# A block pair with 16 experts on one core: the router taken chunk by chunk from unscaled rows, the first expert job written out, and the high half's buffer given back after the high pass

## What is computed

```python
h = h + (g_conv * y_conv + g_sgu * y_sgu) @ w_out          # output projection
t = rms_norm(h, norm_ffn_g)                                # t = h / rms(h) * gain
p_group = softmax(t @ w_rg + b_rg)                         # 4 groups
pg, g_idx = top_k(p_group, 1)
exp_logits = t @ w_re + b_re                               # 16 experts, 4 in a group
sel = exp_logits of the chosen group; the best 2 of softmax(sel), normalised
gate = pg * those weights
hid = silu(t @ w_gate[e]) * (t @ w_up[e])                  # D_EXPERT = 512
y = sum over e of (hid * gate[:, e]) @ w_down[e]
out = rms_norm(h + y, norm_final_g)
```

## Time and profile before

| what | value |
|---|---|
| median of 3 runs | 2387.46 us (2387.45 to 2388.37) |
| the profiled execution, its time | 2387.44 us |
| its span | 2385.7 us |
| TensorE busy | 2328.2 us (98%) |
| VectorE busy | 1625.7 us (68%) |
| ScalarE busy | 1219.7 us (51%) |
| GpSimd busy | 185.5 us (8%) |
| mean granted TensorE clock | 0.984 |
| bytes moved | 510.90 MB, mean 214 GB/s |

### The profile page before, as it was taken

How to read it: one execution, slowest core, us unless ns; L and a number is a source line. 1 busy time by engine, 2 the same in 40 slices (tenths; PEclk the granted TensorE clock), 3 DMA queues, 4 the chain that set the end, 5 groups by cost and what they waited for, 6 DMA issues and landing times.

```text
span 2385.7 us, 35385 instructions
## 1 busy us (share of the span) xinstructions
PE 2328.2 (98%) x12313; PEld 1985.9 (83%) x12313; DVE 1625.7 (68%) x1904; ACT 1219.7 (51%) x1217; POOL 185.5 (8%) x71
## 2 busy tenths in 40 slices
PE   9999899999999999999999999999979999999997
PEld 9999688888888878888888888887867877778776
DVE  2999666555566554445586655575558888888887
ACT  4443346444444434444543544443446776767666
POOL 4676001000000000000100000000000000000000
PEclk9999899999999999999999999999979999999999
DMA  7655256667667655554676666654529989899895
GB/s 195 168 151 173 65 193 172 184 191 192 185 186 193 188 164 193 193 193 159 197 213 190 173 187 186 183 175 171 193 73 342 359 306 371 322 343 349 316 370 209
DMA packets 445235, 510.90 MB, mean 214 GB/s; under 512 B 12252, under 2 KB 407156, under 8 KB 410100
## 3 DMA queue, kind: packets, MB, share of 16 engines
q1 hardware_dynamic: 443812, 504.30, 65.6%
q0 software_dynamic: 1104, 5.78, 0.7%
q10 hardware_dynamic: 272, 0.20, 0.0%
HBM read 508.15 MB, written 2.10 MB: 214 GB/s over the span
## 4 chain that ended last, share of the span: by engine, by line
PE 93%; DVE 3%; ACT 2%; issue 2%; DVEq 0%; ACTq 0%; POOL 0%; POOLq 0%
PE ps L1925 24%; PE ps L1843 16%; PE ps L1930 13%; PE ps L2109 9%; PE ps L2125 7%; PE ps L2113 5%; PE ps L1753 3%; PE ps L1754 3%; PE ps L1776 2%; PE ps L2001 2%; ACT whi L553 1%; PE ps L1856 1%; PE ps L2090 1%; DVE wlo L988 1%; PE ps L1693 1%
## 5 line engine op out<-in xcount | busy, mean ns | idle before, releaser
L988 DVE TENSOR_TENSOR wlo<-raw,whi 128x2048 fp32r<-128x2048 f32 x440 | 1007.3, 2290 | 291.2 <-ACT whi L553 290.0
L553 ACT ACTIVATE whi<-raw 128x2048 fp32r<-128x2048 f32 x476 | 911.6, 1916 | 536.3 <-PE ps L1843 214.8
L1925 PE MATMUL ps<-xT,whi 128*128 128x512 f32 x2656 | 638.1, 391 | 5.2 <-DVE xT L1390 4.3
L1925 PEld LDWEIGHTS ps<-xT,whi 128*128 128x128 f32 x2656 | 487.7, 189 | 99.5 <-issue 4.4
L1930 PEld LDWEIGHTS ps<-xT,wlo 128*128 128x128 f32 x2656 | 343.2, 191 | 14.3
L1930 PE MATMUL ps<-xT,wlo 128*128 128x256 f32 x2656 | 347.4, 283 | 0.0
L733 ACT ACTIVATE wk<-ps 128x256 f32<-128x256 f32 x184 | 68.8, 383 | 451.5 <-PE ps L1930 451.5
L1843 PE MATMUL ps<-whi,act 128*128 128x512 f32 x1120 | 270.4, 394 | 2.8 <-ACT act L650 2.8
L2109 PE MATMUL ps<-whi,moe_r 128*128 128x512 f32 x1024 | 258.5, 395 | 6.0 <-ACT whi L553 6.0
L1843 PEld LDWEIGHTS ps<-whi,act 128*128 128x128 f32 x1120 | 213.5, 191 | 50.4 <-ACT act L650 3.7
L2109 PEld LDWEIGHTS ps<-whi,moe_r 128*128 128x128 f32 x1024 | 191.8, 189 | 49.8 <-ACT whi L553 7.6
(11 more groups left out here) (285 smaller groups left out, 1838.0 us busy)
## 6 DMA issues: line engine op xcount, KB each, us to landing
raw<-in_w_in SPq DMA_DIRECT2D x72, 1024.0 KB, 5.5
raw<-in_w_exp_gate SPq DMA_DIRECT2D x64, 1024.0 KB, 4.8
raw<-in_w_exp_up SPq DMA_DIRECT2D x64, 1024.0 KB, 4.8
raw<-in_w_exp_down SPq DMA_DIRECT2D x64, 1024.0 KB, 4.8
raw<-in_ffn_w_gate SPq DMA_DIRECT2D x44, 1024.0 KB, 5.6
raw<-in_ffn_w_up SPq DMA_DIRECT2D x44, 1024.0 KB, 5.5
raw<-in_ffn_w_down SPq DMA_DIRECT2D x44, 1024.0 KB, 4.8
raw<-in_conv_w_in SPq DMA_DIRECT2D x32, 1024.0 KB, 6.0
```

What stands on the lines that cost most here:

```text
L553: fn(whi[:, s % 2, :], raw[:, s % RING, :], ACT.Copy).then_inc(hi_ready, 1)
L988: V.tensor_tensor(wlo[:, s % 2, :], raw[:, s % RING, :], whi[:, s % 2, :], ALU.subtract).then_inc(lo_ready, 1)
L1925: mm(ps[:, bank, :], whi[:, s % 2, at:at + P], xT5[:, k0 + k, :], start=(k == 0), stop=False)
```

## The change

- The router's weights are multiplied once by the gain of the norm (`wr_scaled`; the gain comes as columns with one more small transfer at the start). The logits are then made from the unscaled `h`, and the reciprocal root is applied to the 20 logits with the bias, on VectorE, after them.
- `h` is turned chunk by chunk (`turn_tokens`) into the bank just added; those of token block 0 and the first logits stand between the chunks of the output projection's last pair (`between`). Copies of block 0 are VectorE's, of block 1 ScalarE's. Squares are taken by chunks.
- GpSimd multiplies `h` by the gain into `tmp` (eight chunks); ScalarE and VectorE split these into `tH` and `tL` by chunks with the reciprocal root as a scale (`token_hi`, `token_lo`), at four places of their order.
- `fill(6)` puts six 128-column matmuls of ones after the logits and six after the ranks.
- The first job is written out before the loop, which now is `Fori(1, jobs)`. It has no scatter, no result to split, no `take`. Its gathers use four banks, and its first four panels start as each chunk of `xg` is there. The experts' choice is spread between its panels; the loop's count is computed after panel 8 and loaded after the job. The body common to all jobs is `job_rest`.
- `expert_hi` takes the place of `hi` for all expert panels but the first two of a job: it waits for the end of the high pass of panel s-2 (new semaphore `whi_used`) and for its `lo`, not for `mm_done`. `expert_lo` waits in addition for `mm_done` of panel s-2, whose low half it overwrites.

```diff
+            def expert_hi(n, s):
+                a.wait_ge(whi_used, n + (s - 1 - MOE))
+                a.wait_ge(lo_ready, n + (s - 1 - B))
+                a.wait_ge(raw_in[s % RING], n * 4 + (16 * (s // RING) + 16))
+                fn(whi[:, s % 2, :], raw[:, s % RING, :], ACT.Copy).then_inc(hi_ready, 1)
+            def expert_lo(n, s):
+                v.wait_ge(mm_done, n + (s - 1))
+                lo(n, s)
...
 in_panel:
                 for o in range(2):
                     for k in range(4):
-                        mm(ps[:, bank, :], xg[:, o, 4 * q + k, :], whi[:, s % 2, k * DE:(k + 1) * DE],
-                           start=(q == 0 and o == 0 and k == 0), stop=False)
+                        i = mm(ps[:, bank, :], xg[:, o, 4 * q + k, :], whi[:, s % 2, k * DE:(k + 1) * DE],
+                               start=(q == 0 and o == 0 and k == 0), stop=False)
+                i.then_inc(whi_used, 1)
                 pe.wait_ge(lo_ready, n + (s + 1 - B))
...
 GpSimd:
-            pool.wait_ge(mm_done, MOE)
+            pool.wait_ge(mm_done, G)
             pool.iota(...); pool.memset(SelT ...)
+            pool.wait_ge(gain_in, 96)
+            for t in range(TOK):
+                for c in range(NC):
+                    pool.wait_ge(add_done, 16 + t * NC + c + 1)
+                    pool.tensor_tensor(tmp[:, t, c * BANK:(c + 1) * BANK], h[:, t, c * BANK:(c + 1) * BANK],
+                                       gB[:, c * BANK:(c + 1) * BANK], ALU.mult).then_inc(xn_ready, 1)
...
 ScalarE, router:
+            for c in range(NC):
+                row_square(0, c)
+            for c in range(NC):
+                row_square(1, c)
+                if c == 0:
+                    row_root(0)
+                if c == NC - 1:
+                    row_root(1)
+                a.wait_ge(tt_turned, NC + c + 1)
+                fn(tiles[:, 4 * c:4 * c + 4, P:2 * P], ps[:, 4 + c, :]..., ACT.Copy).then_inc(tt_ready, 1)
+            token_hi(0)
+            token_hi(1)
+            hi(MOE, 0)
+            token_hi(2)
+            gathered(0, 0, FIRST_ROWS[0])
+            token_hi(3)
+            gathered(0, 1, FIRST_ROWS[1])
+            gathered_hi(0, 0, FIRST_TURN[0])
+            hi(MOE, 1)
+            gathered(0, 2, FIRST_ROWS[2])
+            gathered_hi(0, 1, FIRST_TURN[1])
+            gathered(0, 3, FIRST_ROWS[3])
+            gathered_hi(0, 2, FIRST_TURN[2])
+            expert_hi(MOE, 2)
+            gathered_hi(0, 3, FIRST_TURN[3])
+            expert_hi(MOE, 3)
+            expert_hi(MOE, 4)
+            (two Exp) expert_hi(MOE, 5)
+            silu_gate(MOE + 4)
+            expert_hi(MOE, 6)
+            expert_hi(MOE, 7)
+            job_rest(0, MOE)
...
 VectorE, router:
+            for c in range(NC):
+                row_add(0, c)
+            for c in range(NC):
+                row_add(1, c)
+                if c == 1:
+                    row_sum(0)
+                if c == 2:
+                    row_scale(0)
+                v.wait_ge(tt_turned, c + 1)
+                V.tensor_copy(tiles[:, 4 * c:4 * c + 4, 0:P], ps[:, c, :]...).then_inc(tt_first, 1)
+            row_sum(1)
+            row_scale(1)
...
+            for t in range(TOK):
+                V.scalar_tensor_tensor(out=lg[:, t, :], in0=ps[:, t, 0:NL], scalar=st[:, RS + t:RS + t + 1], in1=brow[:, :],
+                                       op0=ALU.mult, op1=ALU.add)
             (mask)
+            token_lo(0)
             (ranks, slots, select(0))
+            token_lo(1)
+            token_lo(2)
+            gathered_lo(0, 0, FIRST_TURN[0])
+            lo(MOE, 0)
+            token_lo(3)
+            gathered_lo(0, 1, FIRST_TURN[1])
+            lo(MOE, 1)
+            gathered_lo(0, 2, FIRST_TURN[2])
+            gathered_lo(0, 3, FIRST_TURN[3])
+            expert_lo(MOE, 2)
             chosen_logits()
+            expert_lo(MOE, 3)
             chosen_experts()
+            expert_lo(MOE, 4)
+            expert_lo(MOE, 5)
+            silu_gate(1)
             chosen_gates()
+            expert_lo(MOE, 6)
+            expert_lo(MOE, 7)
+            expert_lo(MOE, 8)
+            overflow()
+            job_rest(0, MOE)
...
 TensorE:
+            row_stage(G, S_G, KT, first_rows)      # first_rows(c): turn_tokens(0, c); from c = 2 on logits(0, c - 2)
+            turn_tokens(1, 0)
+            turn_tokens(1, 1)
+            turn_tokens(1, 2)
+            logits(0, 2)
+            turn_tokens(1, 3)
+            logits(0, 3)
+            for c in range(NC):
+                i = logits(1, c)
+            i.then_inc(logits_done, 1)
+            fill(6)
             (ranks)
+            fill(6)
...
-            for b in range(4, 8):
-                open_bank(b)
             pe.wait_ge(tri_ready, 3)
             pe.wait_ge(sel_ready, 2)
-            gather(0, 0)
-            for q in range(4):
-                if q < 3:
-                    gather(0, q + 1)
-                turn_rows(0, q)
+            gather(0, 0, FIRST_ROWS[0])
+            gather(0, 1, FIRST_ROWS[1])
+            turn_rows(0, 0, FIRST_TURN[0])
+            gather(0, 2, FIRST_ROWS[2])
+            turn_rows(0, 1, FIRST_TURN[1])
+            first_panel(0)                         # waits for xg chunk 0 alone
+            gather(0, 3, FIRST_ROWS[3])
+            turn_rows(0, 2, FIRST_TURN[2])
+            first_panel(1)
+            turn_rows(0, 3, FIRST_TURN[3])
+            first_panel(2)
+            first_panel(3)
+            in_panel(MOE, 4, 0, 1)
+            in_panel(MOE, 5, 1, 1)
+            slots()
+            in_panel(MOE, 6, 2, 1)
+            in_panel(MOE, 7, 3, 1)
+            job_rest(0, MOE)
             pe.wait_ge(jobs_ready, 1)
             jobs = nc.tensor.value_load(sti[0:1, 0:1], ...)
-            with pe.Fori(0, jobs) as jb:
+            with pe.Fori(1, jobs) as jb:
```

More of the change, by code:

```diff
@@ L878, in gathered, with row_square, row_root @@
-            def gathered(count, q):
+            def row_square(t, c):
+                a.wait_ge(add_done, 16 + t * NC + c + 1)
+                fn(big[:, (8 + t * NC + c) * BANK:(9 + t * NC + c) * BANK], h[:, t, c * BANK:(c + 1) * BANK], ACT.Square,
+                   accum_out=st[:, SSQ + t * NC + c:SSQ + t * NC + c + 1]).then_inc(ssq_ready, 1)
+            def row_root(t):
+                a.wait_ge(rsum_ready, t + 1)
+                root(st[:, SS + t:SS + t + 1], st[:, RT + t:RT + t + 1], 1.0 / D, st[:, EPS_AT:EPS_AT + 1])
@@ L916, in _ @@
             jobs = nc.scalar.value_load(sti[0:1, 0:1], min_val=GROUPS, max_val=GROUPS + 1)
-            with a.Fori(0, jobs) as jb:
+            with a.Fori(1, jobs) as jb:
                 n = jb * JOB + MOE
@@ L1501, in _ @@
             v.wait_ge(tri_ready, 2)
-            step(V.tensor_copy(iota, iota.bitcast(I32)))
+            own.mark(V.tensor_copy(iota, iota.bitcast(I32)))
+            v.wait_ge(bias_in, 32)
+            v.wait_ge(rscale_ready, 2)
             v.wait_ge(logits_done, 1)
-            step(V.tensor_copy(lg, ps[:, 0, 0:2 * 32].rearrange("p (t c) -> p t c", t=2)[:, :, 0:NL]))
+            for t in range(TOK):
+                own.mark(V.scalar_tensor_tensor(out=lg[:, t, :], in0=ps[:, t, 0:NL], scalar=st[:, RS + t:RS + t + 1], in1=brow[:, :],
+                                                op0=ALU.mult, op1=ALU.add))
+            own.wait(v)
             step(V.reduce_max(mx, lg[:, :, 0:GROUPS], AX_X))
@@ L1517, in _ @@
             step(V.tensor_scalar(rank, rank, 1.0, None, ALU.add))
-            step(V.tensor_tensor(mx, inlow, rank, ALU.mult))
-            step(V.tensor_tensor(slot[:, :, 0:GROUPS], ohg, bc(mx, GROUPS), ALU.mult))
+            step(V.tensor_tensor(low, inlow, rank, ALU.mult))
+            step(V.tensor_tensor(slot[:, :, 0:GROUPS], ohg, bc(low, GROUPS), ALU.mult))
             select(0)
-            step(V.tensor_tensor(mx, rank, mx, ALU.subtract))
-            step(V.tensor_scalar(zz, inlow, float(P), float(-P), ALU.mult, ALU.add))
@@ L1850, in row_panel, with last_row_pair @@
                 all_banks(0, wlo).then_inc(mm_done, 1)
-            def last_row_pair(n, step):
+            def last_row_pair(n, step, between=None):
                 def part(s, o, w, t, chunks):
@@ L1877, in last_row_pair, with row_stage @@
                     i.then_inc(mm_done if c == NC - 1 else tok_done, 1)
-            def row_stage(n0, step, count):
+                    if between:
+                        between(c)
+            def row_stage(n0, step, count, between=None):
                 with pe.Fori(0, (count - 4) // 4) as r:
@@ L1885, in row_stage @@
                     row_panel(n0 + count - 4, s, step + count - 4 + s + 1)
-                last_row_pair(n0 + count - 4, step + count - 4)
+                last_row_pair(n0 + count - 4, step + count - 4, between)
             row_stage(B, S_B, KT)
```

421 lines of the change are left out of this document (231 added, 190 removed).

## The result

The changed kernel took 2358.36 us (median of 4 runs, 2356.11 to 2359.92) against 2387.55 us for the kernel before on the same chip (4 runs, 2387.45 to 2388.37): a ratio of 0.9874 [0.986, 0.9887]. Forecast were 2359.5 and 2354 to 2369. The span of the profiled execution fell from 2385.7 to 2358.2 us.

The account below looks back on a forecast made before the run. TensorE, busy 98% of the span, was taken to lose time in the serial router and in expert-stage stalls. 20.5 + 8.5 - 0.9 = 28.1 us off 2387.44 gave 2359.3, written 2359.5; range 2354 to 2369.

Parts of the forecast that it names:

- Logits 12.7 us earlier: Router by chunks: logits end at 1740.3 instead of 1753.04, at full clock, with 0.92 us per group of four logits matmuls.
- Mask and rank 5.5 instead of 5.9, first gather 13.1 earlier: After the logits: mask and rank take 5.5 us (ends 5.0 and 7.0), so the first gather comes at 1745.8.
- First gather to panel 7: 35.2 us with VectorE the bound: First job's start: panel 7 ends 22.5 us earlier at full clock, 20.5 carried for half-clock stretches (ends 17 and 23).
- Release 8.5 of 10.2: Expert stage: freeing the high buffer after the high pass recovers 8.5 of 10.2 us of in-job stalls (ends 0 and 10.2).
- The border keeps its plain order, 2.2 each: Between jobs: the stall of 2.2 us at each of three borders stays.
- Transfers have time to spare: Expert stage: earlier requests would move 380 GB/s instead of 373; slots have time to spare, as no ACT wait names DMA.
- Rival (a): Expert stage: the release buys nothing, since transfers or DVE take its place; 2368 us, chance 0.20 before 0.02 taken from it.
- Trip count at the first border: 0.9 lost: First job border: loading the loop's trip count there costs 0.9 us (ends 0 and 2).
- Overflow count hidden; additional waits free: First job and expert panels: the count costs 1.6 us only if uncovered; added waits on ACT and DVE unlikely to cost.
- rival (d): Expert panels: one more wait each on ACT and DVE makes the kernel slower, from 0.40 us per wait; chance 0.03.
- The sum: Whole kernel: 20.5 for router and first panels, plus 8.5 for the release, minus 0.9 for the trip count: 28.1 us.
- rival (c): Whole kernel: all runs at full clock with all stalls gone, 22.9 + 10.2 - 0.5; 2355 us, chance 0.10.

Follow-up runs that it names:

- x0: The changed kernel run again, unchanged: 2356.82 us, ratio 0.987 to the kernel before.
- x8: The changed kernel with the first expert panel waiting for all four gathered chunks, ScalarE's last gathered copy moved ahead of panel 2's: 2360.28 us (three runs).
- x4: The changed kernel with the overflow count moved from behind panel 8 to near the end of the first job: 2358.59 us, ratio 0.9874.
- x10: The changed kernel, unchanged, run a third time: 2358.54 us, ratio 0.9872 to the kernel before.
- x2: The kernel before with only the early release of the high buffer, for all expert panels but a job's first two: 2380.21 us, ratio 0.9963.
- x5: The changed kernel with the early release also for the first two panels of jobs 2 to 4: 2356.21 us, ratio 0.9866.
- x11: The changed kernel with a one-column exponential put between the written-out first job and the loop: 2360.23 us, ratio 0.9887.

## Why the prediction was right

- **Logits 12.7 us earlier.** 12.63 from A. Two errors cancel in it: a group of four logits matmuls takes 0.80 us at full clock and not 0.92, and the last five groups took 4.83 us, 0.8 more than that, since the clock fell before their end. In absolute time the gain was 11.8, since A itself came 0.83 later. In the changed kernels A lies anywhere from 1722.75 to 1726.56; I had put the additions ahead of the router at 0 to 0.7 and can't tell them from this scatter.
- **Mask and rank 5.5 instead of 5.9, first gather 13.1 earlier.** 7.1 and 11.45 in the profile of after, 5.64 and 13.0 in x0. The size hangs on the clock: a fill group takes 2.74 us at half, stands in the queue ahead of the ranks, and ends 0.8 us after these could have begun; the second ends some 0.6 us after the selection matrix is ready. I had left the fill out of the sum. At full clock (1.44 us in x8) it is hidden.
- **First gather to panel 7: 35.2 us with VectorE the bound.** 35.4 in after, 34.6 in x0, and the chain of that stretch names `lo` and VectorE's small steps. Panel 7 at 20.5 earlier was 20.58; at nearly full clock, in x0, 23.0 against the 22.5 worked out for it. Two microseconds for the clock was right in size, and its place too: TensorE busy, clock half. The second half stretch of after, within 1767 to 1771, falls where TensorE waits for VectorE and costs nothing: x4 and x10, without it, end panel 7 as late. The Trainium skill (TensorE: Matmul & The Clock Gate, What's actually happening), read as a rule on the busy share, would have given 22.5; the 1741 and 1746 windows, 0.50 at a busy share of 1.00, contradict that reading again.
- **Release 8.5 of 10.2.** Alone it gave 8.75 by x2's trace (9.1 in time). In the changed kernel undoing it costs 10.5. The period is down to 33.12 us, against 33.08 of work, with low passes at 0.91. The stretch behind it, 1999.53 to 2046.79, takes 47.26 us against 47.1 of work and 47.86 before, so 0.2 of stall is left there.
- **The border keeps its plain order, 2.2 each.** Wrong by 0.45 per border, a gain: the table load. The kernel before's chain had it ahead of panel 0's copy at each border, and I counted it into the 2.2 us of "plain order". The move of the exponential was in the diff; I had priced the instruction and not what it does to the loop behind it. Both together, 2.36 + 2.62 + 2.57 + 2.67 = 10.2 in x0, happen to be my upper end. In the profile of after they came to 7.75, because job 1 gained nothing.
- **Transfers have time to spare.** This is the step that failed. It rested on a kernel whose jobs took 148.1; at 145.5 a period asks for 380 GB/s, which is what the windows show at a DMA share of 0.99, so after the dry start behind the router the ring has next to no reserve, and in three of ten profiled executions job 1 pays 2.6 us or more. I had named a wait of ScalarE for a transfer as what would show me wrong; 17.0 us of it stood in the profile. Rival (a) had that mechanism, but for all jobs; it lives in one.
- **Trip count at the first border: 0.9 lost.** Nothing was lost: 7.67 us at the border with the load, 7.66 at the one without. Of the border's 2.2 us the table load was 0.45, and x5's early release takes 0.77 more.
- **Overflow count hidden; additional waits free.** x4 bears out the first. For the second, twelve panels and a turn are 33.08 us of work, and the period is 33.12 with a wait more on ACT and on DVE per panel: rival (d) did not happen, and the stage lengthened by at most 0.04 us in twelve panels. A wait's own price is not shown by that, since VectorE had 0.29 us per panel to spare by the prediction's own sum.
- **The sum.** 20.6 + 7.75 - 0.8 = 27.5 against 28.1. Job 1's loss and A's 0.8 are set off by the table loads and by the 0.9 that was not to be paid; so the closeness of the total owes something to errors of opposite sign. With job 1 undisturbed and a short half clock the case is near rival (c)'s 2355 (x0's profiled execution took 2356.33), and executions lie between the two.

## What to carry to other kernels

When a double buffer is read by two passes and only the second pass's end gives it back, look for low passes a few tenths too long at regular places: releasing it after the pass that reads it last gave back nearly all the stall, at no cost of the second semaphore that the time shows. On ScalarE, ask of a moved function what table it leaves behind for the loop that follows. Then ask again what the transfers can spare, with the new period and after each stretch in which the ring ran dry: "no wait names a DMA" holds for the old period alone. Judge an edit inside a loop by the loop's period in the trace, here equal to 0.05 us between executions, when the total scatters by 3 us.

## What the runs showed that I had not expected

- Where the last function ahead of a loop was an exponential and the last one in it a sigmoid, each turn of the loop had two table loads of 1.28 us (before, x2, x11); with a sigmoid last ahead of it there was none (after, x0). The Trainium skill (ScalarE activation tables: per-element evaluation and per-set limits, Table sets in the compiler and the runtime) says that the back end places the loads per block; these traces fit it, with a load at the head of each turn and one at its sigmoid.
- The same router code on the same chip (x5 and x8, for one pair) ran for 3.4 or 10.2 us at the half clock in different executions, TensorE being busy in both (nine executions have the fill and the new router; four and five of them); with it panel 7 moves by 2.5 us (57.75 against 60.21).
- Twelve 128-column matmuls of ones put in to keep TensorE occupied came too late to hold the clock: it fell in the 1740 window of after and the first of them ran from 1741.22, all at 0.50 (1741 and 1746 windows); without them panel 7 ended at the same time within the scatter.
- The changed kernel's three sets of runs scatter by 3.8, 0.95 and 4.2 us. That is not all its own: the kernel before repeats within 0.9 us beside the result (2387.45 to 2388.37), but its other four sets scatter by 1.5 to 3.3 (2387.70 to 2390.98 the widest). What the changed kernel adds is seen in the profiles: 2.5 us with the half clock, and 2.6 to 3.8 us in job 1 in the three executions of ten where the ring fell behind.
